# Expert weights in units of 2 MB, token rows of three expert pairs fetched by indirect DMA, and a scatter in three parts

## The reference, cut to what matters

```python
def _ec_moe(h, router, w1, w3, w2):     # N_EXPERTS 16, cap 64, D 1024, EXPERT_FF 1024
    probs = jax.nn.softmax(jnp.einsum('bnd,de->ben', h, router).astype(jnp.float32), axis=1)
    gates, idx = lax.top_k(probs, cap)                  # every expert takes its 64 best tokens
    xs = h[bidx, idx]
    a = jnp.einsum('becd,edf->becf', xs, w1)
    g = jnp.einsum('becd,edf->becf', xs, w3)
    y = jnp.einsum('becf,efd->becd', jax.nn.silu(a) * g, w2) * gates[..., None].astype(h.dtype)
    return jnp.zeros_like(h).at[bidx, idx].add(y)
```

## Time and profile before

| | |
|---|---|
| median of three runs | 2468.9 us |
| span of the profiled execution | 2464.2 us |
| PE (TensorE) busy | 2299.2 us, 93% |
| DVE (VectorE) busy | 944.2 us, 38% |
| ACT (ScalarE) busy | 496.8 us, 20% |
| POOL (GpSimd) busy | 0.2 us |
| DMA | 557.00 MB, mean 226 GB/s |
| weights of the experts | 384 DMAs of 1024 KB |
| expert stage of layer 0, first up matmul to end of the last down | 485.4 to 940.3 us |
| the same of layer 1 | 1198.7 to 1653.7 us |

### The profile page before, as it was taken

One profiled execution on the slowest core, in us unless ns is written; L12 is line 12 of the kernel. 1 busy time (PEld: TensorE's weight loads), 2 busy tenths in 40 slices (PEclk: granted clock), 3 DMA queues, 4 the chain that ended last, 5 costly groups with the idle time before them and its releaser, 6 DMA issues.

```text
span 2464.2 us, 30598 instructions
## 1 busy us (share of the span) xinstructions
PE 2299.2 (93%) x12972; PEld 1162.4 (47%) x12972; DVE 944.2 (38%) x1668; ACT 496.8 (20%) x885; POOL 0.2 (0%) x4
## 2 busy tenths in 40 slices
PE   6999999799999998988799999999999999999697
PEld 1354345444444443436444444436885447644445
DVE  4648653301111113675211111126762446323474
ACT  1357100211111112021211111111112321113501
POOL 0000000000000000000000000000000000000000
PEclk9999999899999999999899999999999999999899
DMA  7613425499999993661799999972221221122151
GB/s 279 225 35 103 154 94 189 196 422 421 421 421 421 421 421 149 229 245 56 305 421 421 420 422 422 420 295 86 86 101 53 78 70 37 41 83 73 52 188 69
DMA packets 97012, 557.00 MB, mean 226 GB/s; under 512 B 13577, under 2 KB 14089, under 8 KB 40363
## 3 DMA queue, kind: packets, MB, share of 16 engines
q1 hardware_dynamic: 90432, 538.77, 55.7%
q10 hardware_dynamic: 6444, 16.28, 1.7%
HBM read 544.53 MB, written 10.49 MB: 225 GB/s over the span
## 4 chain that ended last, share of the span: by engine, by line
PE 80%; DVE 13%; ACT 3%; DMA 3%; issue 1%; ACTq 0%; SPq 0%; DVEq 0%
PE bank L215 78%; DMA fast_w<-in_w_in 2%; PE bank L218 2%; DVE residual L1589 1%; DMA wmod<-in_w_mod 1%; DVE wring L1494 0%; DVE squares L1555 0%; DVE max L1493 0%; ACT scores_t L3042 0%; ACT squares L1549 0%; DVE fast_s L1955 0%; DVE fast_s L1954 0%; DVE fast_s L1956 0%; DVE fast_s L1953 0%; DVE residual L536 0%
## 5 line engine op out<-in xcount | busy, mean ns | idle before, releaser
L215 PE MATMUL bank<-normed,wring 128*128 128x512 f32 (+2 forms) x1392 | 580.5, 604 | 3.9 <-ACT normed L1766 2.1
L215 PE MATMUL bank<-experts,wring 128*64 128x512 f32 x1792 | 393.1, 593 | 4.2 <-ACT wring L1529 4.2
L215 PEld LDWEIGHTS bank<-normed,wring 128*128 128x128 f32 (+1 forms) x1392 | 229.5, 182 | 284.9 <-issue 277.4
L1555 DVE TENSOR_TENSOR squares<-squares,bank 128x512 f32<-128x512 f32 x32 | 22.0, 688 | 651.0 <-ACT squares L1549 651.0
L215 PEld LDWEIGHTS bank<-experts,wring 128*64 128x64 f32 x1792 | 127.2, 137 | 253.6 <-issue 249.1
L215 PE MATMUL bank<-experts,hs_t 128*64 128x512 f32 x896 | 209.4, 594 | 1.5 <-ACT hs_t L1570 1.5
L215 PE MATMUL bank<-give_t,y 128*128 128x512 f32 x256 | 128.6, 621 | 10.2 <-DVE residual L1589 5.9
L215 PEld LDWEIGHTS bank<-experts,hs_t 128*64 128x64 f32 x896 | 67.3, 137 | 123.3 <-issue 119.9
L215 PE MATMUL bank<-pick,h_tm 128*128 128x128 f32 x1024 | 122.2, 279 | 2.4 <-DVE pick L1506 2.4
L215 PEld LDWEIGHTS bank<-pick,h_tm 128*128 128x128 f32 x1024 | 119.5, 196 | 2.6 <-issue 2.6
L1589 DVE SCALAR_TENSOR_TENSOR residual<-bank,mods,residual 128x512 f32<-128x512 f32 x128 | 96.0, 750 | 56.9 <-PE bank L215 51.2
(11 more groups left out here) (568 smaller groups left out, 2403.3 us busy)
## 6 DMA issues: line engine op xcount, KB each, us to landing
experts<-in_exp_w SPq DMA_DIRECT2D x336, 1024.0 KB, 18.1
normed<-in_exp_w SPq DMA_DIRECT2D x48, 1024.0 KB, 18.8
wring<-in_w_in SPq DMA_DIRECT2D x52, 512.0 KB, 3.7
wmod<-in_w_mod SPq DMA_DIRECT2D x16, 1024.0 KB, 7.5
residual<-in_w_mod SPq DMA_DIRECT2D x16, 1024.0 KB, 5.8
cf_wmod<-in_w_mod SPq DMA_DIRECT2D x16, 1024.0 KB, 5.7
fast_w<-in_w_in SPq DMA_DIRECT2D x30, 512.0 KB, 4.2
wring<-in_cf_w SPq DMA_DIRECT2D x20, 512.0 KB, 3.5
```

The lines of the kernel that those rows point to most:

```text
L215: return self.nc.tensor.matmul(out, lhsT, rhs, start=start, stop=stop, skip_group_check=True)
L1555: k.vec(v.tensor_tensor(m.hs[:, e, :], m.hs[:, e, :], k.bank[3 - 2 * e][:, :], ALU.mult), f"{m.name}.hs{i}.{e}")
```

## The change

- The weights come in units of 2 MB, 128 partitions x 16 KB, through a ring of 8 slots (7 of their own, one in the whole of `k.H`), 96 units for a layer. Three units are issued ahead of layer 0's fence, four ahead of layer 1's. The host lays the weights out accordingly.
- ScalarE writes the token-major rows `ht` to a tensor in DRAM, in four DMAs of 512 KB, while it routes.
- New: `places_tensor` multiplies `pm` by the probabilities and, as a 17th column, by the tokens' numbers. So each slot knows its token and its gate; `places_vector` copies both out.
- For the last `NFETCH` = 3 pairs GpSimd fetches the 128 chosen rows (4 KB each) from DRAM by an indirect DMA, and the gather is 4 transposes in each half instead of 16 matmuls (32 records). The other five pairs gather as before, but wait for the gate copies.
- `pt` is made by one VectorE instruction: token number equal to the slot's token, times the gate. The give matrix, its transposes and the copy on ScalarE are gone.
- The scatter of a pair is done in three parts: chunks 0 to 3 between the up parts, 4 and 5 behind the first hidden transposes, 6 and 7 behind the second. The hidden transposes use banks 2 and 3 and no longer wait for the adds.

```diff
--- before.py
+++ after.py
@@ -34,7 +34,8 @@
 SLOPES = [2.0 ** (-8.0 * (h + 1) / 4) for h in range(4)]
-NRING = 15
+NRING = 8
+NFETCH = 3
@@ -1332,23 +1333,25 @@
-NEARLIER = 5
+NEARLIER = 3
...
-        ring = at.sb("experts" + L, [P, NRING - 2, 2, FF])
+        ring = at.sb("experts" + L, [P, NRING - 1, 4, FF])
         self.ht = at.sb("h_tm" + L, [P, NT, D])
-        self.pb = at.sb("probs" + L, [P, NT, NE])
+        self.told = at.sb("probs" + L, [P, NT, NE + 1])
+        self.pb = self.told[:, :, 0:NE]
...
-        self.pet = at.sb("probs_e" + L, [NE, T])
...
-        self.pg = at.sb("give" + L, [P, NT, 2, CAP])
-        self.pt = at.sb("give_t" + L, [P, T])
+        self.pt, self.tok = k.R, k.mrow
+        self.place = k.nc.alloc_sbuf_tensor_at("place" + L, [P, 1], mybir.dt.uint32, offset=at.next)
+        at.next += 32
+        self.gate = at.sb("gate" + L, [P, 2, 2])
@@ -1359,11 +1362,11 @@
-        self.ring = [ring[:, n, :, :] for n in range(NRING - 2)]
-        self.ring += [k.H[:, 4 * n:4 * n + 4, :].rearrange("p (k c) t -> p k (c t)", k=2) for n in range(2)]
+        self.ring = [ring[:, n, :, :] for n in range(NRING - 1)]
+        self.ring += [k.H[:, :, :].rearrange("p (k c) t -> p k (c t)", k=4)]
-        up = [(i, q, e, j) for i in range(NPAIR) for e in range(2) for j in range(4) for q in (1, 3)]
-        down = [(i, 2, e, j) for i in range(NPAIR) for j in range(4) for e in range(2)]
+        up = [(i, q, e, j) for i in range(NPAIR) for e in range(2) for j in range(2) for q in (1, 3)]
+        down = [(i, 2, e, j) for i in range(NPAIR) for j in range(2) for e in range(2)]
@@ -1380,7 +1383,7 @@
     i, q, e, j = m.order[n]
-    src = k.a[f"exp_w{q}"][m.layer].rearrange("e j p (k f) -> e j p k f", k=2)[2 * i + e, j]
+    src = k.a[f"exp_w{q}"][m.layer].rearrange("e j p (k f) -> e j p k f", k=4)[2 * i + e, j]
@@ -1465,6 +1468,7 @@
                                scale=m.rs[:, n:n + 1]), f"{name}.ht{n}.{h}")
+        s.dma_start(k.a[f"rows{m.layer}"][n * P:(n + 1) * P, :], m.ht[:, n, :]).then_inc(*k.up(f"{name}.rows{n}", f"{name}.kept{n}", 16))
@@ -1481,11 +1485,14 @@
-    k.vec(v.memset(m.pet[:, :], 1.0))
+    k.vec(v.memset(m.pt[:, :], 1.0))
...
+    k.vec(v.tensor_tensor_scan(m.tok[:, :], m.pt[:, :], m.pt[:, :], -1.0, ALU.mult, ALU.add))
+    for n in range(NT):
+        k.vec(v.tensor_copy(m.told[:, n, NE:NE + 1], k.con("dist", 384 - P * n, 1)))
     v.wait_ge(*k.at(f"{name}.probs"))
@@ -1493,7 +1500,7 @@
-    k.vec(v.tensor_tensor_scan(wk[:, 0, :], m.pet[:, :], wk[:, 1, :], 0.0, ALU.mult, ALU.add))
+    k.vec(v.tensor_tensor_scan(wk[:, 0, :], m.pt[0:NE, :], wk[:, 1, :], 0.0, ALU.mult, ALU.add))
@@ -1506,21 +1513,66 @@
+def places_tensor(k, m, i):
+    t = k.nc.tensor
+    t.wait_ge(*k.at(f"{m.name}.pick{i}"))
+    for n in range(NT):
+        ins = k.mm(k.bank[7][:, 0:NE + 1], m.pm[:, n, :, :].rearrange("p e c -> p (e c)"), m.told[:, n, :], n == 0, n == NT - 1)
+    ins.then_inc(*k.up("tensor", f"{m.name}.found{i}"))
+def places_vector(k, m, i):
+    v, b, g = k.nc.vector, k.bank[7], m.gate[:, i % 2, :]
+    v.wait_ge(*k.at(f"{m.name}.found{i}"))
+    k.vec(v.tensor_copy(m.place[:, :], b[:, NE:NE + 1]), f"{m.name}.place{i}")
+    k.vec(v.tensor_copy(g[:, 0:1], b[:, NE:NE + 1]))
+    for e, r in enumerate(HALVES):
+        k.vec(v.tensor_copy(g[r, 1:2], b[r, 2 * i + e:2 * i + e + 1]), f"{m.name}.gate{i}" if e else None)
 def give_vector(k, m, i):
-    po = m.pb[:, :, 2 * i:2 * i + 2].unsqueeze(3).broadcast_to([P, NT, 2, CAP])
-    k.vec(k.nc.vector.tensor_tensor(m.pg[:, :, :, :], m.pm[:, :, :, :], po, ALU.mult), f"{m.name}.give{i}")
+    g = m.gate[:, i % 2, :]
+    k.vec(k.nc.vector.tensor_scalar(m.pt[:, :], m.tok[:, :], g[:, 0:1], g[:, 1:2], ALU.is_equal, ALU.mult), f"{m.name}.pt{i}")
+def fetched(i):
+    return i >= NPAIR - NFETCH
+def rows_of(m, i):
+    return m.ht[:, i - (NPAIR - NFETCH), :]
+def rows_pool(k, m):
+    g = k.nc.gpsimd
+    for n in range(NT):
+        g.wait_ge(*k.at(f"{m.name}.kept{n}"))
+    for i in range(NPAIR - NFETCH, NPAIR):
+        g.wait_ge(*k.at(f"{m.name}.place{i}"))
+        if i == NPAIR - NFETCH:
+            g.wait_ge(*k.at(f"{m.name}.gather{i - 1}.1"))
+        g.indirect_dma_start(rows_of(m, i), None, k.a[f"rows{m.layer}"], bass.IndirectOffsetOnAxis(m.place[:, 0:1], 0)).then_inc(
+            *k.up(f"{m.name}.fetched{i}", f"{m.name}.xr{i}", 16))
 def gather_tensor(k, m, i, h):
-    t, bank = k.nc.tensor, k.bank
-    t.wait_ge(*k.at(f"{m.name}.pick{i}"))
+    t, b = k.nc.tensor, k.bank[6 + h]
+    t.wait_ge(*k.at(f"{m.name}.gate{i}"))
+    if fetched(i):
+        t.wait_ge(*k.at(f"{m.name}.xr{i}"))
     for c in range(4 * h, 4 * h + 4):
-        for n in range(NT):
-            ins = k.mm(bank[6 + c // 4][:, (c % 4) * P:(c % 4 + 1) * P], m.ht[:, n, c * P:(c + 1) * P], m.pm[:, n, :, :],
-                       n == 0, n == NT - 1)
-        if c % 4 == 3:
-            ins.then_inc(*k.up("tensor", f"{m.name}.gather{i}.{c // 4}"))
+        dst = b[:, (c % 4) * P:(c % 4 + 1) * P]
+        if fetched(i):
+            ins = k.turn(dst, rows_of(m, i)[:, c * P:(c + 1) * P])
+        else:
+            for n in range(NT):
+                ins = k.mm(dst, m.ht[:, n, c * P:(c + 1) * P], m.pm[:, n, :, :], n == 0, n == NT - 1)
+    ins.then_inc(*k.up("tensor", f"{m.name}.gather{i}.{h}"))
@@ -1533,19 +1585,19 @@
-    for j in range(4):
+    for j in range(2):
         for q, w in ((0, 1), (1, 3)):
...
-            for c in range(2):
+            for c in range(4):
...
@@ -1557,24 +1609,22 @@
     t, bank = k.nc.tensor, k.bank
-    if i:
-        t.wait_ge(*k.at(f"{m.name}.add{i - 1}.{6 + e}"))
     t.wait_ge(*k.at(f"{m.name}.hs{i}.{e}"))
     for c in range(4):
-        ins = k.turn(bank[4 + e][:, c * P:(c + 1) * P], m.hs[:, e, c * P:(c + 1) * P])
+        ins = k.turn(bank[2 + e][:, c * P:(c + 1) * P], m.hs[:, e, c * P:(c + 1) * P])
...
-def scatter_tensor(k, m, i, behind=None):
+def scatter_tensor(k, m, i, chunks=range(KD), behind=None):
...
-    for c in range(KD):
+    for c in chunks:
...
-def scatter_vector(k, m, i):
+def scatter_vector(k, m, i, chunks=range(KD)):
...
@@ -1593,12 +1643,12 @@
-    for j in range(4):
+    for j in range(2):
...
-        for c in range(2):
-            kk = 2 * j + c
+        for c in range(4):
+            kk = 4 * j + c
@@ -1609,27 +1659,30 @@
     route_tensor(k, m)
+    places_tensor(k, m, 0)
     gather_tensor(k, m, 0, 0)
     gather_tensor(k, m, 0, 1)
     for i in range(NPAIR):
+        more = i + 1 < NPAIR
         t.wait_ge(*k.at(f"{m.name}.xs{i}.1"))
         up_tensor(k, m, i, 0)
+        if more:
+            places_tensor(k, m, i + 1)
         if i:
-            scatter_tensor(k, m, i - 1)
-        t.wait_ge(*k.at(f"{m.name}.give{i}"))
-        for n in range(NT):
-            ins = k.turn(bank[7][:, n * P:(n + 1) * P], m.pg[:, n, :, :].rearrange("p e c -> p (e c)"))
-        ins.then_inc(*k.up("tensor", f"{m.name}.given{i}"))
+            scatter_tensor(k, m, i - 1, range(4))
         up_tensor(k, m, i, 1)
         hidden_tensor(k, m, i, 0)
-        if i + 1 < NPAIR:
+        if i:
+            scatter_tensor(k, m, i - 1, range(4, 6))
+        if more:
             gather_tensor(k, m, i + 1, 0)
         hidden_tensor(k, m, i, 1)
-        if i + 1 < NPAIR:
-            t.wait_ge(*k.at(f"{m.name}.pt{i}"))
+        if i:
+            scatter_tensor(k, m, i - 1, range(6, KD))
+        if more:
             gather_tensor(k, m, i + 1, 1)
         down_tensor(k, m, i)
-    scatter_tensor(k, m, NPAIR - 1, behind)
+    scatter_tensor(k, m, NPAIR - 1, behind=behind)
     fence(k, m.name, "tensor")
@@ -1638,18 +1691,22 @@
     pick_vector(k, m, 0)
+    places_vector(k, m, 0)
     give_vector(k, m, 0)
     for i in range(NPAIR):
         if i + 1 < NPAIR:
-            v.wait_ge(*k.at(f"{m.name}.gather{i}.1"))
+            if not fetched(i):
+                v.wait_ge(*k.at(f"{m.name}.gather{i}.1"))
             pick_vector(k, m, i + 1)
         up_vector(k, m, i, 0)
+        if i + 1 < NPAIR:
+            places_vector(k, m, i + 1)
         if i:
-            scatter_vector(k, m, i - 1)
-        if i + 1 < NPAIR:
-            v.wait_ge(*k.at(f"{m.name}.given{i}"))
-            give_vector(k, m, i + 1)
+            scatter_vector(k, m, i - 1, range(4))
         up_vector(k, m, i, 1)
+        if i:
+            scatter_vector(k, m, i - 1, range(4, KD))
+            give_vector(k, m, i)
     if ahead:
@@ -1663,8 +1720,6 @@
-        s.wait_ge(*k.at(f"{m.name}.given{i}"))
-        k.act(s.copy(m.pt[:, :], k.bank[7][:, :]), f"{m.name}.pt{i}")
@@ -1706,12 +1761,11 @@
     k.nc.sync.wait_ge(*k.at(f"ad.row{NEARLY + 7}"))
-    for n in range(2, 8):
+    for n in range(1, 4):
         unit_sync(k, experts, n)
     next(blocks)
     k.nc.sync.wait_ge(*k.at(f"ad.row{len(ROWS) - 1}"))
-    for n in range(2):
-        unit_sync(k, experts, n)
+    unit_sync(k, experts, 0)
     all_steps(blocks)
@@ -3308,6 +3362,9 @@
+    for m in (experts0, experts1):
```

(21 more changed lines are left out.)

## The result

Over 20 executions each, the changed kernel has a median of 2475.5 us and the kernel before of 2469.25 us: ratio 1.0023, 95% interval [1.0013, 1.0032], some 6 us slower. I had forecast 2467, 2 us faster than the median of before. Executions of one kernel spread over some 12 us (2468.5 to 2480.8 after, 2462.6 to 2475.1 before). The profiled one of after took 2477.6 us with a span of 2476.3, so 1.3 us lie around the span and not the 4.7 that I had read from before; the rest of those 4.7 was only that the profiled execution of before was one of its quicker ones. (Every later execution whose span is on record lies 1.2 to 1.6 us over it.) So 12.1 us between the two spans are about 6 us between the medians.

What follows compares the result with a forecast made beforehand. PE bounds by under 3 us a layer, then the weights' arrival: last landing 931.7 + 6.9 + 0.9 = 939.5 against 940.3, -1.6 for both layers. 2464.2 - 1.6 + 4.7 = 2467 us, range 2449 to 2486.

Steps and rivals of the forecast that it cites:

- What bounds: Expert layers: PE bounds now by under 3 us a layer; after the change the weights' arrival bounds the last pairs.
- The price of a fetch: Indirect row fetches beside the weights: 1.3 us each on the DMA queue, 3.9 a layer.
- Rival D: Fetched rows land late and PE waits for them: about +10 us a layer at 40 us, 2487; chance 0.07.
- Rival B: Large weight runs cost only their bytes, 4.78 us a unit: 2443, or 2455 for half the gain; chance 0.19.
- E: Indirect DMA does not spare PE the gather: +1 us a layer, 2470; chance 0.03.
- The unit: Weight stream: a 2 MB unit takes 4.92 us, 2% less than before, between 4.78 and 5.04.
- The release: First ring slot freed at 492.0: 487.4 before, plus 2.9 for the later start and 1.7 for larger units.
- the start: Start of a layer, scan, copies and places ahead of the first gather: +2.9 us, bounds 1.5 to 5.
- a price on the clock: End of a layer: PE at half clock after a wait loses 1.7 us; half taken, 0.9.
- The tail: Behind the last landing: 6.9 us for the last down half plus 0.9 for the clock.
- Rival C: Nothing gained on larger runs, or fetches dear: 5.02 us a unit, layer 8.8 us longer, 2485; chance 0.18.
- the margin: Sum of a layer: end at 939.5 against 940.3, so -0.8 us a layer, -1.6 for both.

Runs made afterwards that it cites:

- the runs with equal tails: Changed kernel, first gather ahead of places, scan behind first pick: with 2 MB units, last ones in halves, ratio 0.9965; with all units of 1 MB, 0.9995.
- with the hole filled: 11 idle matmuls in PE's hole while VectorE ranks tokens; ratios to the kernel before: changed kernel 1.0009, kernel before 0.9977, with three repairs 0.9939.
- fetches twice: Changed kernel with each row fetch issued a second time into an unused tile, transposes waiting for both; ratio 1.0050 to the kernel before.
- gather first: Changed kernel with each layer's first gather ahead of the places matmuls, waiting for pick alone; ratio 0.9996 to the kernel before.
- the halves: Changed kernel with the last pair's second down units arriving as four halves of 1 MB; ratio 1.0002 to the kernel before.
- three repairs: Changed kernel with first gather ahead of places, scan and token copies behind first pick, last down half's weights in 1 MB halves; 2459.0 us, ratio 0.9965.

## Why the prediction was wrong

The forecast of a layer was 39.1 to the release, 7.2 from issue to landing, 432.5 for 87 units with fetches, and 7.8 behind: 486.6 us. Layer 0 took 43.1 + 7.4 + 434.6 + 8.9 = 494.0, layer 1 39.7 + 7.4 + 434.7 + 8.9 = 490.7. Both lie over it, by 7.4 and 4.1 us, and these 11.5 are most of the 13.7 by which the span passed my 2462.6; 1.8 more lie ahead of the first fence. The medians ask for less: from 2469.25 to 2475.5 instead of 1.6 us down is 3.9 us a layer over the forecast, which is what layer 1 shows.

- **What bounds** was right: the weights end the layer, PE waits for them 15.6 and 17.3 us in a layer, as foretold, and the gain of fetched gathers vanishes in these waits. The slices said 427 where I had 429.
- **The price of a fetch** was right, 1.0 to 1.3 us each against 1.3. Rival D is out: rows are issued at 736.2, land 11 us later and are used at 754.7. Rival B is out, and E too. The Trainium skill's page DMA: Bandwidth & Descriptors (Latency and other measured facts) says that engines 7 and 15 are usually slower and guesses at the descriptor rings of such DMAs. No run here tells the engines apart; as a dearer unit it would have shown, and doubling the fetches added only 1.0 us each.
- **The unit** was mis-sized: 4.92 taken; without fetches landings are 4.95 us apart (2 x 2.476). PE was the bound there, but that is still the queue's own pace: its single steps have a median of 4.89 us, as in after. A few longer steps, 3.8 to 4.3 us a layer in all, in before as well, make up the mean; what lengthens them isn't shown. 0.03 x 87 = 2.6 us a layer, and 2.1 net of the 0.6 that I had allowed for a dry queue. I had taken 2% off for 16 KB runs; the runs with equal tails show 1.5% (2.533 against 2.496 us for each MB), the medians of single steps 1.6% (4.894 against 2 x 2.486).
- **The release** was the step that failed most in layer 0, by 4.0 us, and by 0.6 in layer 1. I summed +2.9 for the start and 1.7 for the larger unit. Layer 1 came out 5.3 over before, and with the hole filled both layers do, within 0.4: 0.9 for the scan, as summed, 1.7 for the unit, as summed, and 2.8 for places and copies ahead of the gather, where I had 2.0; most of that miss is that the places matmuls ran at half clock (1.86 us, 0.96 at full). Layer 0 had 3.3 us more: behind a hole of 11.65 us (10.78 before) half clock lasted 17.1 us in place of 10.2 and came back for 3.4 at the first up (13.7 us and no such stretch in layer 1). The gather took 10.29 us where the earlier trace rows had 8.75 (1.5 us), and the up matmuls ahead of the release lost 1.7. I had put a price on the clock at the end of the layer, and none at its start, though the half clock there was in the trace of before too. With the hole filled the change stays as much slower than before, so this explains layer 0 of the trace and not the sign.
- **The tail**: 8.9 for 7.8. I took half of a loss of 1.7 us; the hole of 2.66 to 2.74 us brought the half clock in both layers, whole, and from the landing to the first matmul and in the pipe 0.3 more go. Of the eight layers that end with whole units of 2 MB behind fetched rows (after, fetches twice, gather first, after with the hole filled) seven have this tail of 8.9. Only layer 1 with the gather first escaped: its last matmuls behind such a hole ran at full clock, and the tail was 7.2. Half of the loss was too small a share:

```profile
1654.70 0.61 PE L216 MATMUL bank<-experts,hs_t 128*64 128x512 f32 x1 [2.71 <-DMA normed<-in_exp_w]
```

- **Rival C** named 4 us a layer as the point from which slower wins. The sum went past it, but only some 2 of it by C's mechanism. No rival of mine held the start. And since the medians differ by 6 us and not by the 12 of the spans, the time stayed inside the bound of 0.3% that I took for "same" and the range held it; that the sign was wrong, the interval shows.
- Behind these stands the margin: -0.8 us a layer came from a sum whose start alone had bounds 3.5 us apart, and each of the three terms, all of one sign, was enough to turn it, taken as the mean of the two layers (2.3, 2.1 and 1.1 us). The price of the start and of the unit, both too low, are the steps that failed whatever the clock did.

What isn't settled: all executions together gain less than the traces by the halves (5 us for 8) and by leaving out the fetches (1 to 5 for 8), and more by the gather in front (6.7 for 4.3); and where before gains by idle matmuls. The first three differences are of the size by which single executions scatter.

## What to carry to other kernels

When the transfers of a stage are the bound, what counts is only the chain from the stage's start to the first freed slot, the bytes, and the work behind the last landing: a larger unit makes the bytes cheaper and both ends longer, so give it small units at the end. Keep preparation for later steps (here token numbers and gates) off the chain to the first release. A hole of ten microseconds in PE can be paid twice, once as a hole (10.7 to 11.7 us here) and once at half clock from its middle on (10.2 to 17.1 us); cheap idle matmuls in it were worth 0.23% of before and 0.26% of the kernel with three repairs; the 0.14% of after is within the noise.

## What I had not expected of the hardware

- **The same program releases its first slot at times some 3 us apart.** In eight of the fourteen profiled executions the two layers differ by 2.4 to 3.6 us (43.1 and 39.7 in after, 40.4 and 42.8 with halves, 37.5 and 34.5 with the hole filled), in the others by under 0.7. It isn't bound to the layer: three times layer 1 is the later. It is the clock: in all eight the later layer, and it alone, has 3.4 us at half clock at the first up (492.9 to 496.3 in after), and the half clock behind the hole reaches further into the gather; in the other six both layers have that stretch or neither has. An execution's mean granted clock goes with its time: of the 20 of after the three shortest (2468.5 to 2469.4 us) have 0.976, the three longest (2478.5 to 2480.8) 0.970 to 0.972.
- **16 KB runs save 1.5%** of the transfer time under a full queue (2.496 us for each MB, against 2.533 with 8 KB runs).
- **An indirect DMA of 128 rows of 4 KB** lands 11 us after its issue under a full weight queue, takes GpSimd 0.9 to 1.1 us, and costs the weights beside it 1.0 to 1.3 us.
